# Shift row moved from VectorE to ScalarE and GpSimd, and two norms' sums taken as f32r products of a high and a low part

## The reference

```
# first block
h = rmsnorm(x, norm_mix_g);  u = h @ w_in                    # 2048 x 12288
...                                                            # convolution and HGRN2 branches -> m
x = x + m @ w_o
gate = sigmoid(rmsnorm(x, ple_norm_g) @ w_ple_gate)
x = x + gate * (p @ w_ple_proj)
x = rmsnorm(x, final_norm_g)
# second block
shift, scale, g = split(silu(c) @ w_ada + b_ada, 3)
h = rms_norm(x, norm_gain) * (1 + scale) + shift
proj = h @ w_in2                                               # q_r first, then the others
...                                                            # retention and dilated attention -> y
x = x + g * (y @ w_out2)
out = rms_norm(x, final_gain)
```

## Time and profile before

| | us |
|---|---|
| median of three runs | 2528.23 |
| lowest and highest | 2527.05, 2528.45 |
| profiled execution, its own time | 2527.45 |
| its span in the profile | 2526.2 |
| PE busy | 2513.8 |
| DVE busy | 1366.9 |
| ACT busy | 943.3 |
| POOL busy | 77.9 |

### The profile page before, as it was taken

How to read it: one execution, slowest core, us unless ns; L and a number is a source line. 1 busy time by engine, 2 the same in 40 slices (tenths; PEclk the granted TensorE clock), 3 DMA queues, 4 the chain that set the end, 5 groups by cost and what they waited for, 6 DMA issues and landing times.

```text
span 2526.2 us, 31905 instructions
## 1 busy us (share of the span) xinstructions
PE 2513.8 (100%) x13050; PEld 2088.4 (83%) x13050; DVE 1366.9 (54%) x2224; ACT 943.3 (37%) x1282; POOL 77.9 (3%) x64
## 2 busy tenths in 40 slices
PE   9999999999999999999999999999999999999998
PEld 8888888888888888888888888888888888888888
DVE  7547744467534555555443263585356555664425
ACT  6643335333332222322232253443344344444323
POOL 0000000000000000000001103200000000000000
PEclk9999999999999999999999999999999999999999
DMA  5322233322334666666443223235322334343424
GB/s 191 111 89 84 84 100 93 92 84 84 93 99 150 218 219 210 224 206 214 150 159 109 95 97 100 92 92 185 91 76 75 95 109 112 102 118 112 163 92 158
DMA packets 196850, 317.70 MB, mean 126 GB/s; under 512 B 47904, under 2 KB 52256, under 8 KB 195680
## 3 DMA queue, kind: packets, MB, share of 16 engines
q1 hardware_dynamic: 195904, 314.11, 40.0%
q0 software_dynamic: 224, 1.15, 0.1%
q10 hardware_dynamic: 576, 0.42, 0.1%
HBM read 298.84 MB, written 8.39 MB: 122 GB/s over the span
## 4 chain that ended last, share of the span: by engine, by line
PE 100%; DVE 0%; ACT 0%; issue 0%
PE bank L342 94%; PE bank L1369 1%; PE bank L1371 1%; PE bank L1370 1%; PE bank L765 0%; PE bank L838 0%; PE bank L749 0%; PE bank L841 0%; PE bank L798 0%; PE bank L1756 0%; DVE X L2164 0%; PE bank L1869 0%; PE bank L436 0%; PE bank L441 0%; PE bank L442 0%; PE bank L790 0%
## 5 line engine op out<-in xcount | busy, mean ns | idle before, releaser
L342 PE MATMUL bank<-XH,WH 128*128 128x512 f32 (+1 forms) x2880 | 1106.6, 386 | 0.0
L342 PE MATMUL bank<-XH,WL 128*128 128x512 f32 (+1 forms) x2880 | 1101.8, 385 | 0.0
L342 PE MATMUL bank<-XL,WH 128*128 128x512 f32 (+1 forms) x2880 | 1101.2, 384 | 0.0
L392 DVE TENSOR_TENSOR WL<-RAW,WH 128x1024 fp32r<-128x1024 f32 x443 | 546.3, 1234 | 771.1 <-ACT WH L369 770.7
L369 ACT CAST WH<-RAW 128x1024 fp32r<-128x1024 f32 x443 | 466.0, 1053 | 1083.7 <-PE bank L342 1079.9
L342 PEld LDWEIGHTS bank<-XH,WL 128*128 128x128 f32 x2880 | 540.7, 188 | 108.4 <-DVE WL L392 0.3
L342 PEld LDWEIGHTS bank<-XH,WH 128*128 128x128 f32 x2880 | 540.9, 188 | 107.2 <-issue 0.5
L342 PEld LDWEIGHTS bank<-XL,WH 128*128 128x128 f32 x2880 | 540.9, 188 | 106.7 <-issue 0.5
L342 PE MATMUL bank<-WH,XL 128*128 128x512 f32 x384 | 149.4, 389 | 0.0
L342 PE MATMUL bank<-WL,XH 128*128 128x512 f32 x384 | 149.4, 389 | 0.0
L342 PE MATMUL bank<-WH,XH 128*128 128x512 f32 x384 | 149.4, 389 | 0.0
(11 more groups left out here) (310 smaller groups left out, 1747.3 us busy)
## 6 DMA issues: line engine op xcount, KB each, us to landing
RAW<-in_w_in SPq DMA_DIRECT2D x303, 512.0 KB, 3.7
AST<-in_w_ada SPq DMA_DIRECT2D x192, 256.0 KB, 4.0
RAW<-in_w_out SPq DMA_DIRECT2D x40, 512.0 KB, 3.7
RAW<-in_w_o SPq DMA_DIRECT2D x32, 512.0 KB, 3.6
RAW<-in_w_gate SPq DMA_DIRECT2D x32, 512.0 KB, 3.6
RAW<-in_w_a SPq DMA_DIRECT2D x16, 512.0 KB, 4.1
RAW<-in_w_b SPq DMA_DIRECT2D x16, 512.0 KB, 4.2
PT<-ZT SPq DMA_DIRECT2D x256, 32.0 KB, 1.9
```

The source lines that it names most:

```text
L342: ins = nc.tensor.matmul(bank[b][:, cols], l, r[:, cols], start=first, stop=final)
L392: nc.vector.tensor_tensor(WL[:, m % NSPL], RAW[:, m % NRAW], WH[:, m % NSPL].bitcast(F32), ALU.subtract).then_inc(lo.sem, lo.step(m))
```

## The change

1. **Gate norm.** ScalarE casts `AC[:, 0]` to f32r (`PLE_H`), VectorE subtracts (`PLE_L`), and TensorE takes two f32r products. The sum is now a special, so it stands one step later, after 12 matmuls of `proj` 1.
2. **Second norm.** The same for both sums (`ACH`, `ACL`), whose place in TensorE's queue stays. ScalarE's two casts stand between its last rows of `XH`, VectorE's two subtractions between its last rows of `XL`.
3. **Shift row.** ScalarE makes each product of a weight row tile and its shift (`BQ` for the first, then one of four slots `BT`), GpSimd adds them up, and VectorE has none of it. The loads into `RAW` wait for ScalarE's product in place of VectorE's.
4. **Turning the row.** Its four float32 matmuls have 8 columns of ones in place of 128.

```diff
@@ dve_dense
-                if 0 <= m - FIRST["qr", 0] < 8:
-                    yield from shift_dve(m)
...
+    def shift_act():
+        A.wait_ge(dve, (yield dve, "mod"))
+        A.wait_ge(dve, (yield dve, ("gx", 15)))
+        for u in range(8):
+            m = FIRST["qr", 0] + u
+            A.wait_ge(raw[m % NRAW], (yield raw[m % NRAW], m))
+            if u > 1:
+                A.wait_ge(pool, (yield pool, ("bq", 2 * u - 3)))
+            for k in (2 * u, 2 * u + 1):
+                nc.scalar.activation(BT[:, k % 4] if k else BQ[:, :], RAW[:, m % NRAW, k % 2], ACT.Copy,
+                                     scale=MOD[:, k:k + 1]).then_inc(act.sem, act.step(("bt", k)))
+            yield
+            if u > 3:
+                yield
+
+    def shift_pool():
+        for k in range(1, 16):
+            G.wait_ge(act, (yield act, ("bt", k)))
+            if k > 1:
+                G.wait_ge(pool, (yield pool, ("bq", k - 1)))
+            nc.gpsimd.tensor_tensor(BQ[:, :], BQ[:, :], BT[:, k % 4], ALU.add).then_inc(pool.sem, pool.step(("bq", k)))
@@ load_unit
-                Y.wait_ge(dve, (yield dve, ("bq", 2 * (m - NRAW - FIRST["qr", 0]) + 1)))
+                Y.wait_ge(act, (yield act, ("bt", 2 * (m - NRAW - FIRST["qr", 0]) + 1)))
@@ pe
             if g == 0:
-                b, was = special_bank("r_ple", dve, ("r_ple", "m"))
-                T.wait_ge(was[0], (yield was))
-                T.wait_ge(pool, (yield pool, ("acc1", 15)))
-                ones_sum(b, AC[:, 0], ("r_ple", "sum"))
+                turns.specials.append(gate_norm_pe())
...
+    def gate_norm_pe():
+        b, was = special_bank("r_ple", dve, ("r_ple", "m"))
+        T.wait_ge(was[0], (yield was))
+        T.wait_ge(act, (yield act, ("r_ple", "high")))
+        T.wait_ge(dve, (yield dve, ("r_ple", "low")))
+        ones_sum2(b, PLE_H[:, :], PLE_L[:, :], ("r_ple", "sum"))
+        yield
@@ second_norm_pe
-            T.wait_ge(dve, (yield dve, ("acc2", 15, 0)))
-            T.wait_ge(dve, (yield dve, "acc12"))
-            ones_sum(b, AC[:, 1 - n], (key, "sum"))
+            T.wait_ge(act, (yield act, ("acc2", "high", 1 - n)))
+            T.wait_ge(dve, (yield dve, ("acc2", "low", 1 - n)))
+            ones_sum2(b, ACH[:, 1 - n], ACL[:, 1 - n], (key, "sum"))
...
-        T.wait_ge(dve, (yield dve, ("bq", 15)))
+        T.wait_ge(pool, (yield pool, ("bq", 15)))
...
-            ins = nc.tensor.matmul(b[:, t], BQ[:, t], ONES, start=True, stop=True)
+            ins = nc.tensor.matmul(b[:, 128 * i:128 * i + 8], BQ[:, t], ONES[:, 0:8], start=True, stop=True)
@@ act_program, behind the copies of proj 0
+                A.wait_ge(pool, (yield pool, ("acc1", 15)))
+                nc.scalar.copy(PLE_H[:, :], AC[:, 0]).then_inc(act.sem, act.step(("r_ple", "high")))
...
+        turns.chores.append(shift_act())
         turns.specials.append(second_norm_act())
@@ second_norm_act, behind rows 12 and 13 of XH
+                for u, made in ((0, ("acc2", 15, 0)), (1, "acc12")):
+                    A.wait_ge(dve, (yield dve, made))
+                    nc.scalar.copy(ACH[:, u], AC[:, u]).then_inc(act.sem, act.step(("acc2", "high", u)))
@@ second_norm_dve, ahead of rows 14 and 15 of XL
+                for u in range(2):
+                    V.wait_ge(act, (yield act, ("acc2", "high", u)))
...
+                    nc.vector.tensor_tensor(ACL[:, u], AC[:, u], ACH[:, u].bitcast(F32), ALU.subtract
+                                            ).then_inc(dve.sem, dve.step(("acc2", "low", u)))
@@ dve_program, behind proj 0
+                V.wait_ge(act, (yield act, ("r_ple", "high")))
+                nc.vector.tensor_tensor(PLE_L[:, :], AC[:, 0], PLE_H[:, :].bitcast(F32), ALU.subtract
+                                        ).then_inc(dve.sem, dve.step(("r_ple", "low")))
@@ pool_program, behind the squares
+        yield from shift_pool()
```

More of the change, by code:

```diff
@@ L1181, in build @@
     BQ = sb("BQ", [512], F32, W0 + 98688)
+    PLE_H = sb("PLE_H", [512], F32R, W0 + 47104)
+    PLE_L = sb("PLE_L", [512], F32R, W0 + 96256)
+    ACH = sb("ACH", [2, 512], F32R, W0 + 32768)
+    ACL = sb("ACL", [2, 512], F32R, W0 + 36864)
+    BT = sb("BT", [4, 512], F32, W0 + 65536)
     BV = SM[:, 8:12]
@@ L2189, in second_norm_act @@
             yield from xg_feed["act"].upto(n)
+            if n == 14:
+                for u, made in ((0, ("acc2", 15, 0)), (1, "acc12")):
+                    A.wait_ge(dve, (yield dve, made))
+                    nc.scalar.copy(ACH[:, u], AC[:, u]).then_inc(act.sem, act.step(("acc2", "high", u)))
             yield
@@ L2215, in second_norm_dve @@
         for n in (14, 16):
+            if n == 16:
+                for u in range(2):
+                    V.wait_ge(act, (yield act, ("acc2", "high", u)))
+                    if u:
+                        V.wait_ge(dve, (yield dve, "acc12"))
+                    nc.vector.tensor_tensor(ACL[:, u], AC[:, u], ACH[:, u].bitcast(F32), ALU.subtract
+                                            ).then_inc(dve.sem, dve.step(("acc2", "low", u)))
             yield from xg_feed["dve"].upto(n)
```

## The result

| | before | after |
|---|---|---|
| median | 2527.11 us | 2536.77 us |
| lowest to highest | 2526.97 to 2528.45 | 2535.99 to 2537.24 |
| runs | 6 | 6 |
| span of the profiled execution | 2526.2 us | 2535.9 us |

The change makes the kernel slower: 1.0037 of the time before, with a 95% interval of [1.0027, 1.0046]; that is 9.66 us in the medians and 9.7 between the two spans. The prediction said slower, 2534.5 in 2526.5 to 2537.5. The time lies in the range, 2.3 above the forecast.

What follows compares the result with a forecast made beforehand. It took TensorE, busy for the whole span, as the bound; -0.17 - 0.82 - 0.1 + 5.7 + 2.2 = +6.8 on 2527.45 gave 2534.3, and a quarter of 0.78 more made 2534.5 us, range 2526.5 to 2537.5.

Steps and rivals of the forecast that it cites:

- likeliest case: In qr 0 GpSimd's additions hold VectorE, TensorE waits for ACL and its clock falls: 2532 to 2537 us.
- gate norm's sum, and the wait for bank 6: Gate norm: f32r products gain 0.42; proj 2's fourth tile waits 0.25 for ScalarE's late copy of proj 1.
- second norm's two sums: Second norm in qr 0: four f32r products replace the float32 sums, 0.91 instead of 1.73, gain 0.82 us.
- 8 columns: Turning of the shift row: fewer columns in the moving part, gain taken as 0.1 us, from nothing to 0.8.
- wait for `ACL`: Second norm's sums: VectorE and GpSimd alternate, so TensorE starts at 1665.5 instead of 1659.8, waiting 5.7 us.
- clock: TensorE behind the second norm's gap: clock falls to half, costing 2.2 us, or nothing with chance 1 in 5.
- `XL` twice to 1661.0: Step of the second norm's queue count: after acc12 at 1659.7, VectorE runs two XL, 0.6 each, without GpSimd additions between.
- upper bound of 7 us: Most the second norm's wait could be, if GpSimd also gets ahead of the WL and once more of ACL.
- second rival: Second norm: XL and acc12, having a scalar operand, pass running additions; wait 3.4 us, 2530 to 2532, chance 0.14.
- analogy with the start: Size of the clock cost: at half clock the start's 22 records take 0.214 each against 0.113, 2.2 us lost.
- lower bound: Turning of the shift row: no gain from 8 columns if the weight loads already set the distance.
- count without GpSimd: Second norm's queue on VectorE, without GpSimd: sums ready at 1659.0, 0.8 ahead of TensorE, no wait.

Runs made afterwards that it cites:

- run 4: Changed kernel with shift row back on VectorE, ACH casts ahead of ScalarE's next cast, ACL right behind acc12, last four XL rows behind the next WL: 2526.68 us.
- run 3: Changed kernel with each of GpSimd's 15 additions replaced by two memsets of BQ, leaving out the shift row's sum: 2526.68 us, 0.9997.
- run 1: Changed kernel with the second norm's sums as float32 products again, no ACH and ACL, shift row still on ScalarE and GpSimd: 2530.95 us, 1.0015.
- run 2: Changed kernel with the shift row on VectorE again and GpSimd idle in qr 0, new sums and 8 columns kept: 2529.90 us, 1.0010.
- run 5: Changed kernel with ACH casts ahead of ScalarE's next cast and ACL right behind acc12, shift row still on ScalarE and GpSimd: 2532.53 us, 1.0019.
- run 7: Changed kernel with early ACL, gate norm's bank taken before proj 1, last two XL later, GpSimd's first addition waiting for both ACL: 2532.86 us, 1.0021.

## Why the prediction was right, and where its sizes were off

The likeliest case came true, at its upper edge. Its terms against the traces:

| term | predicted | measured |
|---|---|---|
| gate norm's sum, and the wait for bank 6 | -0.42 + 0.25 | -0.42 + 0.36 |
| second norm's two sums | -0.82 | -0.82 |
| 8 columns | -0.1 | 0.0 |
| wait for `ACL` | +5.7 | +8.0 |
| clock | +2.2 | +2.2 |
| sum | +6.8 | +9.3 |

The -0.82 is read in run 4, at full clock. The spans differ by 9.7; the remaining 0.4 is the later start of this execution.

Part of the closeness is luck. The forecast of 2534.5 was the sum of +6.8 on a level of 2527.7, and the kernel before came out at 2527.11. The cost itself was 2.9 too low (9.7 against 6.8), and the lower level hid 0.6 of it.

- **What the profile gave.** All of the mechanism came from one pair of rows of the kernel before, an `XL` of 0.75 and a `WL` of 2.31 beside two additions: exclusion, the one that waits comes next, so with two full queues they take turns. The timelines after show just that, and run 3 shows that it is the additions and not GpSimd's work as such: memsets of the same row hold nothing. The Trainium skill (SBUF — State Buffer, Who interferes with whom) says that a VectorE instruction with two SBUF inputs is shut out by a GpSimd instruction that reads SBUF and not by one that only writes it. The traces agree on both: 5.81 for four additions beside GpSimd's additions, 2.49 beside memsets.
- **The mis-sized term: the wait.** In my count seven GpSimd additions got in ahead of the end of `ACL`. In the trace it was nine, each for about 1.15, which is the 2.3 that were missing (VectorE and TensorE both came some 0.5 later than counted, which cancels). The step that failed is "`XL` twice to 1661.0": I let both run unhindered, because I took GpSimd's queue to be empty after the fifth addition until ScalarE was done with both `ACH`. But ScalarE made the first `ACH` at 1656.31 and the second at 1659.26, half a microsecond earlier than counted, and the sixth addition was ready when the first `XL` ended. VectorE's first addition began ahead of GpSimd's first (1651.72 and 1651.86), where my count had it the other way round, so the fifth stood ahead of the first `XL` and not of `acc12`. The sixth stood ahead of the second `XL` (3.46 for both, not 1.3), the seventh ahead of `WL` (2.29, not 1.1), the eighth and ninth ahead of the two `ACL`. That is one turn less at the front and three more behind `acc12`. The upper bound of 7 us was a slip: its own condition, two more additions of 1.15 ahead of the end of `ACL`, makes 5.7 + 2.3 = 8.0, which is what came.
- **The second rival** (instructions with a scalar operand pass a running addition) is false: `acc12` 1.59 and `XL` 1.73 on average.
- **The clock** was right in size with 2.2. The reason was an analogy with the start. The clock did fall in the gap, 2.3 us into it (3.3 at the program's end). But the cost agrees by luck: it was 22 records at 0.10 in the forecast and 11 products at 0.20 in the trace, and gaps of other lengths cost nothing to 2.9 (last section).
- **The 8 columns.** The lower bound was the true value: the eight records stay 0.113 apart. The Trainium skill (TensorE: Matmul & The Clock Gate, LDWEIGHTS) gives a weight load a time by its own columns, 107 ns for 128. The trace agrees, with 0.91 for eight records at either width.
- **The gate norm.** The mean was forecast at 1455.75 and the logarithm at 1456.5; they started at 1456.12 and 1456.85, which is the 0.37 of the start. The copies of `proj` 1 came 2.4 late and not 2.0, since two rows of `XH` went ahead of them (at 1461.08), and the restart behind the gap costs 0.11 that I had put at nothing.
- **What I hadn't seen:** that the shift row on GpSimd makes TensorE wait even without the new sums (run 1), and that the place of the subtractions costs 2.85 without GpSimd once the shift row is on VectorE (run 2). The prediction's count without GpSimd had no wait there. It also had no `BQ` on VectorE, so run 2 doesn't contradict it, and run 3, which is that case, has `ACL` complete at 1659.3 where the count said 1659.0.

What stays open: the median of run 2 is 0.5 above what its terms give (2.51 above before, against 2.85 - 0.88 = 1.97). In its profiled execution the last product ahead of the gap began at 1660.35, 0.65 later than in run 4 with the same code up to there. Of this 0.48 was there by the 41st product (10.79 against 10.31 us): the later rise of the clock at the start, as above. Whether the median has its 0.5 from there is not shown.

## What to carry to other kernels

An idle GpSimd is not free capacity beside a VectorE that has a deadline: before work is given to it, look in the trace for a moment in which both run two-input instructions in SBUF, and if VectorE's is longer there, price the move at one GpSimd instruction's length for each VectorE instruction that is queued meanwhile, as long as additions are ready. A product made cheaper by splitting its operand needs that operand earlier; look where the split stands in the queue of the engine that makes it (with the shift row on VectorE it was free right behind `acc12` and cost 2.85 behind two `XL`, one `WL` and two `BQ`). And take the bank of a moved product where the old one took it.

## What the runs showed of the hardware

- **Who waits.** A float32 addition of 128x512 on GpSimd (1.29 alone) and VectorE instructions with two inputs in SBUF take strict turns while both have one ready: four additions 5.81 for 2.49, `XL` 6.19 for four, `WL` 2.29 for 1.23. The one-input mean of 0.68 isn't held (run 5: 0.68 beside the ten additions). GpSimd memsets of 0.53 back to back hold nothing.
- **The clock.** All of these are from one execution each, which for runs 1 and 5 was the longest of the eleven. In the changed kernel it fell 2.3 us into the gap of 8.0 and stayed at half for 10.2 us, until 4.6 us behind the restart. After a gap of 2.85 (run 2) it didn't fall. In run 1, with a gap of 2.4, it fell 1.1 us behind the restart for 3.4 us; in run 7, with 3.8, 1.1 behind the restart for 3.4 us; in run 5, with 3.1, it fell in the gap for 6.8 us. So the length of a gap alone didn't tell what it would cost: 0 to 2.9 us on top, and not in the order of the gaps.
- **Small products.** Float32 products of 8 and of 128 columns cost the same, 0.91 for four of them (eight records).
